# Order of the down projection's parts, sums moved behind attention, and four gate tiles of the embedding in two pairs by seven products

## The reference

```python
    x = x + conv_ffn(rmsnorm(x, norm_ffn_gain[i]), ffn_w_up[i], ffn_conv_w[i], ffn_w_down[i])
    gate = jax.nn.sigmoid((x @ ple_w_gate[i]).astype(jnp.float32))
    x = x + (gate * (p[i] @ ple_w_proj[i]).astype(jnp.float32)).astype(dt)
return rmsnorm(x, final_norm_gain)
```

## Time and profile before

| | us |
|---|---|
| median of 3 runs (lowest, highest) | 1231.79 (1231.67, 1231.96) |
| the profiled execution | 1234.19 |
| its span, first to last instruction | 1231.1 |
| PE busy | 1210.4 (98%) |
| DVE busy | 809.7 (66%) |
| POOL busy | 734.0 (60%) |
| ACT busy | 576.4 (47%) |

### The profile page before, as it was taken

One profiled execution on the slowest core, in us unless ns is written; L12 is line 12 of the kernel. 1 busy time (PEld: TensorE's weight loads), 2 busy tenths in 40 slices (PEclk: granted clock), 3 DMA queues, 4 the chain that ended last, 5 costly groups with the idle time before them and its releaser, 6 DMA issues.

```text
span 1231.1 us, 18292 instructions
## 1 busy us (share of the span) xinstructions
PE 1210.4 (98%) x6667; PEld 991.3 (81%) x6667; DVE 809.7 (66%) x1283; ACT 576.4 (47%) x1132; POOL 734.0 (60%) x538
## 2 busy tenths in 40 slices
PE   9999999999999999999999999999999999989997
PEld 7987777787778899987887677788888888888886
DVE  6554427757646877655696565389999989985224
ACT  6365545675634344445635756523232323323444
POOL 8673233253358777845484466457766766976942
PEclk9999999999999999999999999999999999999999
DMA  7332121222122333353241123323333333324422
GB/s 242 103 95 81 56 69 53 59 71 76 53 77 78 102 104 95 106 179 106 59 123 53 52 77 95 95 77 89 96 99 95 94 88 93 86 70 132 122 80 69
DMA packets 62431, 112.21 MB, mean 91 GB/s; under 512 B 6856, under 2 KB 11464, under 8 KB 62344
## 3 DMA queue, kind: packets, MB, share of 16 engines
q1 hardware_dynamic: 62200, 111.06, 31.2%
q10 hardware_dynamic: 144, 0.00, 0.0%
HBM read 108.87 MB, written 2.16 MB: 90 GB/s over the span
## 4 chain that ended last, share of the span: by engine, by line
PE 76%; DVE 18%; issue 3%; ACT 2%; POOL 1%; DMA 1%; SPq 0%; DVEq 0%; POOLq 0%; ACTq 0%
PE pb L1083 17%; PE pb L1084 17%; PE pb L1086 17%; DVE cv L1953 7%; DVE t8s L2016 2%; PE pb L1136 2%; PE pb L1138 2%; PE pb L1137 2%; PE pb L1292 2%; DVE cv L1948 2%; PE pb L1268 2%; PE pb L1145 2%; DVE zf L1941 2%; PE pb L1235 1%; PE pb L1206 1%
## 5 line engine op out<-in xcount | busy, mean ns | idle before, releaser
L2631 POOL TENSOR_TENSOR wlo<-raw,whi 128x512 fp32r<-128x512 f32 (+2 forms) x384 | 546.6, 1442 | 328.1 <-ACT whi L1485 327.7
L1083 PE MATMUL pb<-HH,whi 128*128 128x512 f32 x856 | 346.2, 404 | 0.0
L1084 PE MATMUL pb<-HL,whi 128*128 128x512 f32 x856 | 339.0, 396 | 0.0
L1086 PE MATMUL pb<-HH,wlo 128*128 128x512 f32 x856 | 337.9, 395 | 0.0
L1485 ACT ACTIVATE whi<-raw 128x512 fp32r<-128x512 f32 (+2 forms) x384 | 225.4, 613 | 103.9 <-PE pb L1086 62.3
L1083 PEld LDWEIGHTS pb<-HH,whi 128*128 128x128 f32 x856 | 161.7, 189 | 42.2 <-issue 4.6
L1084 PEld LDWEIGHTS pb<-HL,whi 128*128 128x128 f32 x856 | 161.5, 189 | 38.2 <-issue 2.9
L1086 PEld LDWEIGHTS pb<-HH,wlo 128*128 128x128 f32 x856 | 161.2, 188 | 37.6
L1953 DVE SCALAR_TENSOR_TENSOR cv<-zf,vecs,cv 128x512 f32<-128x512 f32 x88 | 123.8, 1406 | 3.1
L1594 ACT ACTIVATE P<-P,stat 128x256 f32<-128x256 f32 (+3 forms) x96 | 50.5, 527 | 79.6 <-DVE stat L2194 56.1
L2631 POOL TENSOR_TENSOR fl<-cv,fh 128x512 fp32r<-128x512 f32 x22 | 32.6, 1483 | 64.3 <-ACT fh L1862 64.3
(11 more groups left out here) (460 smaller groups left out, 2573.0 us busy)
## 6 DMA issues: line engine op xcount, KB each, us to landing
raw<-in_wall SPq DMA_DIRECT2D x368, 256.0 KB, 2.7
raw<-in_wall SPq DMA_DIRECT2D x8, 260.0 KB, 2.9
X<-in_xT SPq DMA_DIRECT2D x8, 256.0 KB, 5.3
X<-in_xT SPq DMA_DIRECT2D x2, 1024.0 KB, 7.7
outT<-PP SPq DMA_DIRECT2D x8, 256.0 KB, 2.4
raw<-in_wall SPq DMA_DIRECT2D x10, 192.0 KB, 2.4
raw<-in_wall SPq DMA_DIRECT2D x9, 128.0 KB, 2.1
cst<-in_cst SPq DMA_DIRECT2D x1, 832.0 KB, 7.3
```

The lines of the kernel that those rows point to most:

```text
L1083: pe.do.matmul(b, hi, xh[k], start=start, stop=False, skip_group_check=tile[0] == "down")
L1084: pe.do.matmul(b, hi, xl[k], start=False, stop=False, skip_group_check=tile[0] == "down")
L1086: m = pe.do.matmul(b, lo, xh[k], start=False, stop=stop, skip_group_check=tile[0] == "down")
L2631: g.do.tensor_tensor(lo, x, hi.bitcast(F32), ALU.subtract).then_inc(*up(name, point))
```

## The change

1. t_sums(0, 0) moves from behind gm(1, 1) to behind gateA 3; t_parts(0, 0..2) stand behind gateB 0, 1, 2 and t_sums(0, 1), (0, 2) behind gateB 0, 1.
2. The down projection goes by a list `DOWN`: plain tiles 0 to 3, then set 0, tile 4, set 1, tile 5, set 2, tile 6, set 3, tile 7, with banks given by `DOWN_BANK`. The plain tiles 4 to 6 now start their bank, and their set adds to it; tile 7 comes behind its set.
3. The gate tiles of the embedding go in the order 4, 5, (0, 1), (2, 3), 6, 7; the two pairs in seven products, p = NDOWN and NDOWN + 1, with a third group of sums, g = 2 (TS9, TH9, TL9), made of x by t_sums(2, kp) (four 256-wide DVE adds each) and t_parts(2, kp) (ACT, and DVE for the rest). h4's rest of odd d goes to DVE. `EMBED` gives the order of the embeds; the square of a tile is added to acc4 one tile later.

```diff
+NDOWN = NGATE + 4
+EMBED = (4, 5, 0, 1, 2, 3)
+DOWN = [("tile", d) for d in range(4)] + [(x, n) for q in range(4) for x, n in (("pair", q), ("tile", 4 + q))]
+DOWN_BANK = {"tile": (0, 1, 2, 3, 6, 1, 4, 5), "pair": ((4, 5), (7, 0), (2, 3), (7, 0))}
...
@@ pair
             if p < NGATE:
                 self.hold(3 + i, ("acc", p, x))
+            elif p >= NDOWN:
+                self.take_any(("acc", p, x))
@@ stages
                 gm(d, j)
-                if (d, j) == (1, 1):
-                    add("t_sums", 0, 0)
-                if (d, j) == (1, 2):
-                    add("t_parts", 0, 0)
         for t in range(4):
             gate("gateA", "yA", t)
-            if t == 2:
-                add("t_sums", 0, 1)
+            if t == 3:
+                add("t_sums", 0, 0)
         for t in range(4):
             gate("gateB", "yB", t)
+            if t < 3:
+                add("t_parts", 0, t)
             if t < 2:
-                add(("t_parts", "t_sums")[t], 0, 1 + t)
+                add("t_sums", 0, 1 + t)
         while self.background:
             self.step()
-        add("t_parts", 0, 2)
@@ second
+            if d == 7:
+                h4(i)
+                if i in (2, 6):
+                    add("t_sums", 2, i // 4)
+                if i in (8, 12):
+                    add("t_parts", 2, i // 4 - 2)
...
+        for x, n in DOWN:
+            if x == "tile":
+                if n < 7:
+                    self.hold(DOWN_BANK[x][n], ("down", n))
+                self.proj(("down", n), "ffn_dn", P * n, range(8, NPAIR), start=n < 7, stop=n == 7,
+                          between=lambda i: between(n, i))
+                if n == 7:
+                    add("down_out", 7)
+                if n == 5:
+                    add("p_parts")
+                continue
+            for i, t in enumerate(("ab", "cd")):
+                self.hold(DOWN_BANK[x][n][i], ("dn", n, t))
+            if n == 3:
+                self.hold(DOWN_BANK["tile"][7], ("down", 7))
+            self.pair(NGATE + n)
+            add("down_out", 2 * n)
+            if n < 3:
+                add("down_out", 2 * n + 1)
+            if n == 1:
                 add("p_in")
...
         for d in (6, 7):
             add("h4", d)
+            add("t_sums", 2, d - 4)
         for d in range(8):
             take(("pp", d))
             self.proj(("pp", d), "ple_p", P * d, range(2))
             add("pp_out", d)
-        for d in range(6):
+            if d in (4, 7):
+                add("t_parts", 2, 2 + d // 7)
+        for d in (4, 5):
             take(("pg", d, 0))
             self.proj(("pg", d, 0), "ple_g", P * d)
             add("embed", d, 0)
+        for q in range(2):
+            self.pair(NDOWN + q)
+            for d in (2 * q, 2 * q + 1):
+                add("embed", d, 0)
@@ vector, t_sums
+                if g == 2:
+                    v.wait_ge(*at("product7", NDOWN - 1, "S4"))
+                    v.wait_ge(*at("x_down", kp))
+                    v.wait_ge(*at("x_down", kp + 4))
+                    (b11, b12), (b21, b22) = ((xk[n][:, 0:H], xk[n][:, H:T]) for n in (kp, kp + 4))
+                    step(x11, b12, b11, ALU.subtract)
+                    step(x12, b22, b12, ALU.subtract)
+                    v.wait_ge(*last("v_t7"))
+                    step(x22, b22, x11, ALU.subtract)
+                    v.wait_ge(*last("v_t7"))
+                    step(x21, b21, x22, ALU.subtract, ("t_raw", g, kp))
+                    return
@@ vector
+            def h4(d):
+                if d % 2:
+                    v.wait_ge(*at("h4_hi", d))
+                    v.do.tensor_tensor(hl[d], xk[d], hh[d].bitcast(F32), ALU.subtract).then_inc(
+                        *up("v_lo", ("h4_lo", d)))
+
+            def t_parts(g, kp):
+                if g == 2:
+                    v.wait_ge(*at("t_hi", g, kp))
+                    v.do.tensor_tensor(TL9[kp], TS9[kp], TH9[kp].bitcast(F32), ALU.subtract).then_inc(
+                        *up("v_lo", ("t_lo", g, kp)))
@@ vector, embed
-                if 0 < d < 6:
-                    v.wait_ge(*at("sq4", d))
-                    add(acc4, acc4, sq4[(d - 1) % 2], ("sum4_step", d), ("sum4",), name="v_sq")
+                if 1 < n < 7 and half == 0:
+                    v.wait_ge(*at("sq4", EMBED[n - 1]))
+                    add(acc4, acc4, sq4[(n - 2) % 2], ("sum4_step", EMBED[n - 1]), ("sum4",), name="v_sq")
```

More of the change, by code:

```diff
@@ L628, in h4, with between @@
                 add("h4", i // 2)
[L630 to L635, removed]
-        parts_at = {(1, 6): 0, (2, 0): 1, (2, 8): 2, (3, 2): 3}
[L637 to L649, removed]
+        parts_at = {(1, 6): 0, (2, 0): 1, (2, 8): 2, (3, 2): 3}
+        def between(d, i):
+            if (d, i) in parts_at:
+                add("t_parts", 1, parts_at[d, i])
+            if d == 7:
[4 more added lines that the diff above has]
+                    add("t_parts", 2, i // 4 - 2)
+        for x, n in DOWN:
+            if x == "tile":
[17 more added lines that the diff above has]
+            if n == 1:
                 add("p_in")
-            if q == 2:
-                add("p_parts")
         for d in (6, 7):
             add("h4", d)
+            add("t_sums", 2, d - 4)
         for d in range(8):
@@ L927, in build, with place4, before4, gate_tiles @@
         W8 = tensor_at("w8", [P, H], F32, 225152)[:, :]
+        def place4(d, half):
+            return EMBED.index(d) if d < 6 else 2 * half + d
+        def before4(d, half):
+            n = place4(d, half) - 4
+            if n < 0:
+                return "full", ("down", 7)
+            return "embedded", *((EMBED[n], 0) if n < 6 else (n, 0))
+        def gate_tiles(p):
+            if p < NGATE:
+                return [(GMs[(3 * d + j) % 9], gm_free[d, j], ("gm", d, j)) for d, j in PAIRS[p]]
+            return [(t4[place4(d, 0) % 4], before4(d, 0), ("pg_tanh", d, 0)) for d in (2 * (p - NDOWN), 2 * (p - NDOWN) + 1)]
         def sums_at(p):
@@ L1086, in proj @@
                 m = pe.do.matmul(b, lo, xh[k], start=False, stop=stop, skip_group_check=tile[0] == "down")
-                ends = ends and not (tile[0] == "down" and tile[1] < 4)
+                ends = ends and not (tile[0] == "down" and tile[1] < 7)
                 if end or ends:
@@ L1114, in product7 @@
                                   "A22": (("down", 2 * q + 1), 0)}[x]
-                    b, starts = ps(*tile)[:, H * half:H * half + H], half == 0 and (q > 1 or tile[0] == "dn")
+                    b, starts = ps(*tile)[:, H * half:H * half + H], half == 0 and (tile == ("down", 7) or tile[0] == "dn")
                     if starts:
                         free(tile)
-                    if q < 2 and x in ("S4", "A22"):
+                    if x == "S4" or x == "A22" and q < 3:
                         later = [("full", tile)]
@@ L1488, in t_parts @@
                 a.wait_ge(*at("t_raw", g, kp))
[L1489 removed]
+                a.do.activation((TH7, TH8, TH9)[g][kp], (TS7, TS8, TS9)[g][kp], ACT.Copy).then_inc(*up("a_t7", ("t_hi", g, kp)))
             def product7(p, x):
[L1492 removed]
+                if NGATE <= p < NDOWN:
                     return
[L1494 to L1495 removed]
+                (g1, free1, made1), (g2, _, made2) = gate_tiles(p)
                 b = ps("acc", p, "a")[:, 0:H]
@@ L1879, in embed @@
                 c = slice(0, T) if d < 6 else slice(H * half, H * half + H)
-                n = d if d < 6 else 2 * half + d
+                n = place4(d, half)
                 y = t4[n % 4][:, 0:c.stop - c.start]
[L1882 to L1885, removed]
                 if (d, half) == (7, 1):
@@ L2039, in product7 @@
             def product7(p, x):
-                if p >= NGATE:
+                if NGATE <= p < NDOWN:
                     return product8(p, x)
-                one, two = PAIRS[p]
-                g1, g2 = (GMs[(3 * d + j) % 9] for d, j in PAIRS[p])
+                (g1, free1, _), (g2, free2, _) = gate_tiles(p)
+                w = W7 if p < NGATE else W8
                 def from_bank(dst, acc, y, *points):
@@ L2614, in half_out @@
                         mul(PP[d][:, c], PP[d][:, c], r, ("final", d, half))
-            follow({"begin": begin, "split": split, "t_sums": t_sums, "product7": product7, "first": first, "square": square,
+            follow({"begin": begin, "split": split, "t_parts": t_parts, "h4": h4, "t_sums": t_sums, "product7": product7, "first": first, "square": square,
                     "lambda": lam_dots, "norm1": norm1, "kC_out": kc_out,
```

79 lines of the change are left out of this document (47 added, 32 removed).

## The result

The changed kernel takes 1240.47 us (median of 4 runs, 1239.11 to 1241.04), against 1231.86 of the kernel before beside it: ratio 1.0066, 95% interval 1.0053 to 1.0078. It is 8.6 us slower. The forecast was 1235.2 us, +3.4; the time lies above the forecast's own range of 1232 to 1239 and inside the wider one of 1225 to 1241. The profiled execution took 1240.71 us, its span 1238.9.

A forecast was written before the change was run, and what follows sets the result against it. PE, busy 1210.4 of 1231.1 us, was taken as the bound. Attention -3.4, gates +6.6, down projection -6.0, pairs -2.7, their waits and tail +8.9 gave +3.4 on 1231.79: 1235.2 us; own range 1232 to 1239, 8 in 10 1225 to 1241.

The forecast's parts named there:

- the term of the tail: End of embedding: embeds 2 and 3 behind the last pair make PE 1.2 us late before norm4's third sum.
- rival D: Gates and embedding pairs: DVE and POOL block each other for whole operations, 1.71 us a turn; 1242 us; chance 10%.
- Attention, -3.4: Attention: with t_sums(0, 0) gone, the 1.80 us PE wait and 1.6 us of half clock go.
- Gates, +6.6: gateB 3: PE waits for yBlo from POOL, +5.0 us, and the slow clock behind it costs 1.6 us.
- The walk: Queues of ACT, DVE and POOL followed in order from gateA 2; also used for the embedding's waits and the tail.
- cover: gateB 3, trace before: POOL delivers yBlo at 392.74, PE needs it at 393.43; 0.7 us.
- Turns of DVE and POOL, 1.44 us: Gates: one DVE add and one POOL subtraction, slowing each other, take 1.44 us a turn.
- Down projection, -6.0: Down projection: plain tiles between the sets remove all six PE waits in sets 1 and 2; -6.0 us.
- Rival E: Down projection: the tile between doesn't clear the sets, three of six waits stay; 1238 us; chance 5%.
- Embedding up to the half tiles, -2.7 + 7.7: Embedding: two pairs save 2.7 us of PE work; waits in the pairs cost 6.9 us, slow clock 0.8.

The follow-up runs named there:

- the best kernel: Against the kernel with the new down order alone: t_sums(0, 0) moved out of attention to ahead of gateA 0, t_parts(0, 0) behind it; 1223.09 us, 0.9926.

## Why the prediction was right and wrong

The direction came out, and each of the five places was named; the size was short by 5 us, half of it in the term of the tail. The time is nearer rival D's 1242 us than the forecast, but not for D's reason (below).

- Attention, -3.4: measured -3.5 between the two traces, wait and half clock both gone. The half clock may not be in the median execution of the kernel before, see the last section.
- Gates, +6.6: measured +8.0. Wait and place are right, though by two errors that cancelled. The walk had yBlo of gateB 3 done at 398.2; it was 396.36, since ACT's tanh of gateB 3 ran at 389.83 and not at 392.1. And I left out that PE would come 2.5 us earlier (390.95, not the 393.43 of the earlier trace rows), because attention had become faster. A cover read from the trace before has to be moved by what the parts ahead of it gain. The bank wait of 0.4 I didn't have, and the half clock was 1.9 instead of 1.6.
- Turns of DVE and POOL, 1.44 us: in the changed kernel (its timeline of DVE below) four chained adds took 5.71 us beside a busy POOL, 1.43 each, and 1.80 us, 0.45 each, beside an idle one in the best kernel (above). Rival D's turn of 1.71 us did not show. It was worked out from the Trainium skill's page "SBUF — State Buffer", section "Who interferes with whom", which has the loser blocked for the whole instruction; the rows agree that the two slow each other, not with that size.
```profile
379.85 5.71 DVE L2059 TENSOR_TENSOR t7s<-t7s 128x256 f32<-128x256 f32 x4
```
- Down projection, -6.0: -6.6, alone and in the whole change. Rival E fell.
- Embedding up to the half tiles, -2.7 + 7.7 (the 1.2 of the tail left aside) = +5.0: measured +5.2. The 3.2 us wait at A22 was met to the tenth. I had given two things for it, a bank that is short and sums that stand ahead of its read on DVE. The run with another bank shows that the bank is only the place where the wait appears; the trace puts the cause in the sums' order and in a buffer that I had not seen as shared (the sums start after 1.65 us of waiting for POOL).
- The tail, +1.2: measured +3.8, the term that failed most. The walk had one late operand of norm4, the square (1.2 us late, as measured). The sum acc was late too (1.0 us start to start), and the half clock behind the two waits cost 1.6 us, 1.1 of it left at the end: without it, in the kernel with the sums put back, the tail is +2.7 and not +3.8. The steps that failed are the wait for acc and the clock, both put at nothing.

In sum: +1.4 gates, +2.6 tail, +0.2 embedding, -0.6 down, -0.1 attention, +0.5 from the DMA wait at 87 us, on +3.4, gives the 7.4 us between the traces. The medians differ by 8.6; the profiled execution of the kernel before stood 2.4 us over its median, that of the changed one 0.2. So the trace of the kernel before is of one of its longer executions.

## What to carry to other kernels

A step that makes a critical engine wait should move to where its own engine and the partner that it slows are idle, not just out of sight: the same six adds took 3.1 us in one gap and 7 beside a busy POOL, and against the down order alone the kernel was 2.96 us faster with them in that gap, 4.9 slower with them and the steps behind them packed at the gates. Cheaper matmuls (seven products for eight) move work to the engines that prepare operands; here the waits cost more than the saved columns unless enough plain work stood between and behind: a tile of 9.8 us cleared the sets, one of 5.6 us did not clear the pairs. A wait for a bank is to be followed to the read that frees it before banks are reassigned.

## What the runs showed of the hardware

The clock behind a wait is not a function of that wait alone. 1.8 us in attention was followed by half clock in each of the three profiles that have it; 5.4 us for yBlo likewise. But the 3.2 us wait of the second pair was followed by 0.50 in the changed kernel and by 1.00 in the kernel with t_parts(0, 2) behind:
```profile
1196.50:1200.00 3.50, 3.50 (x29) 3.50 (x30) 2.82 (x5) 1.83 (x4) 0.74 (x1) 1.00 0.71 220
```
Executions of that one kernel differ the same way: with a mean clock of 0.998 they took 1234.5 and 1235.1 us, with 0.994 or 0.995 1236.5 to 1237.4, some 2 us. The two waits of 0.9 us at norm4 were followed by 0.50 in the changed kernel and in the one with a tile between the pairs, by 1.00 with the sums put back, with the pair last and with t_parts(0, 2) behind. Part of the 2.4 us by which sums and pairs are worse together may be this; no run here separates it.

The kernel before does it too. Of its 52 executions beside the experiments 15 had a mean clock of 0.997 and took 1233.1 to 1234.2 us, and 33 of the others (0.998, 0.999) took 1231.1 to 1232.9. The profiled one (0.997, 1234.19) is of the first kind, the median of the second. So the half clock of the earlier trace rows is probably missing from the median execution, and the change had 1.6 us less to gain in attention than the trace showed. That would be part of why the medians differ by 8.6 us and the traces by 7.4; no trace of a faster execution was kept, so it isn't shown. A term read from one profile should be held against the spread of the executions.
